# Input projection by Strassen's algorithm: seven products per pair of feature tiles, in three token passes

## What is computed

```python
h = rmsnorm(x, norm_w)
q, k, v, z_a, xbc, z_b, dt_raw, g_a, g_b = jnp.split(h @ w_in, split_points(SPLITS), axis=-1)
...
xbc = causal_conv(xpad, conv_w, conv_b)      # 4 taps along the tokens, then silu
...
dt = jax.nn.softplus(dt_raw.astype(jnp.float32) + dt_bias.astype(jnp.float32))
acs = jnp.cumsum(dt * a, axis=2)
```

## Time and profile before

| | us |
|---|---|
| median of 3 runs | 2437.13 |
| lowest and highest | 2435.5, 2437.49 |
| the profiled execution | 2436.28 |
| its span, first to last instruction | 2434.6 |
| PE busy in the span | 2288.5 (94%) |
| DVE, ACT, POOL busy | 812.7, 831.1, 636.8 |

### The profile page before, as it was taken

How to read it: one execution, slowest core, us unless ns; L and a number is a source line. 1 busy time by engine, 2 the same in 40 slices (tenths; PEclk the granted TensorE clock), 3 DMA queues, 4 the chain that set the end, 5 groups by cost and what they waited for, 6 DMA issues and landing times. The chain is left out here.

```text
span 2434.6 us, 35230 instructions
## 1 busy us (share of the span) xinstructions
PE 2288.5 (94%) x12671; PEld 2062.2 (85%) x12671; DVE 812.7 (33%) x1504; ACT 831.1 (34%) x1925; POOL 636.8 (26%) x547
## 2 busy tenths in 40 slices
PE   6999999999999999999999679999946999996999
PEld 5999999999999999999999668888734878874887
DVE  4211100014444100100000065555517999973221
ACT  5211111124444211221111165555525666742010
POOL 3101011011011011010110055555517767760000
PEclk9999999999999999999999879999976999997999
DMA  4411121111121111211112964444345777735333
GB/s 165 89 72 54 71 71 71 71 70 71 64 77 71 71 70 62 88 54 71 70 71 82 67 165 109 106 120 120 87 118 147 188 195 197 203 104 173 130 129 99
DMA packets 281028, 250.09 MB, mean 103 GB/s; under 512 B 75209, under 2 KB 258361, under 8 KB 273785
## 3 DMA queue, kind: packets, MB, share of 16 engines
q1 hardware_dynamic: 278856, 248.79, 35.8%
q10 hardware_dynamic: 2112, 0.53, 0.1%
HBM read 158.48 MB, written 90.81 MB: 102 GB/s over the span
## 5 line engine op out<-in xcount | busy, mean ns | idle before, releaser
L74 PE MATMUL acc<-h_hi,w_hi 128*128 128x424 f32 (+1 forms) x2280 | 810.5, 355 | 10.2 <-DVE h_lo L561 7.8
L75 PE MATMUL acc<-h_lo,w_hi 128*128 128x424 f32 (+1 forms) x2280 | 807.3, 354 | 0.0
L76 PE MATMUL acc<-h_hi,w_lo 128*128 128x424 f32 (+1 forms) x2280 | 807.0, 354 | 0.0
L74 PEld LDWEIGHTS acc<-h_hi,w_hi 128*128 128x128 f32 x2280 | 430.2, 189 | 24.7 <-DVE h_lo L561 8.6
L332 POOL TENSOR_TENSOR w_lo<-w_raw,w_hi 128x1024 fp32r<-128x1024 f32 x57 | 144.7, 2539 | 1130.5 <-ACT w_hi L374 1130.5
L75 PEld LDWEIGHTS acc<-h_lo,w_hi 128*128 128x128 f32 x2280 | 430.6, 189 | 7.3
L76 PEld LDWEIGHTS acc<-h_hi,w_lo 128*128 128x128 f32 x2280 | 430.2, 189 | 7.3
L399 ACT ACTIVATE row<-acc 128x424 f32<-128x424 f32 (+1 forms) x215 | 112.7, 524 | 825.5 <-PE acc L76 825.4
L597 DVE SCALAR_TENSOR_TENSOR conv_acc<-conv_in,conv_wb,conv_acc 128x424 f32<-128x424 f32 (+2 forms) x216 | 126.1, 585 | 380.9 <-ACT conv_acc L444 373.1
L1120 ACT ACTIVATE a_prob<-a_score,a_neg_max 128x129 f32<-128x129 f32 x264 | 103.3, 398 | 45.9 <-DVE a_neg_max L1259 43.1
L74 PE MATMUL a_o_ps<-a_w_hi,a_at_hi 128*128 128x512 f32 (+1 forms) x272 | 117.0, 430 | 2.0 <-DVE a_branch L1292 2.0
(11 more groups left out here) (218 smaller groups left out, 3045.0 us busy)
## 6 DMA issues: line engine op xcount, KB each, us to landing
proj<-row SPq DMA_DIRECT2D x56, 1056.0 KB, 4.0
w_raw<-in_w_in_dram SPq DMA_DIRECT2D x28, 1024.0 KB, 5.2
s_feat<-proj SPq DMA_DIRECT2D x16, 1280.0 KB, 8.6
s_acs_b<-acs_dram SPq DMA_DIRECT2D x16, 1024.0 KB, 7.5
a_q_diag<-proj SPq DMA_DIRECT2D x66, 128.0 KB, 4.4
a_z<-proj SPq DMA_DIRECT2D x16, 512.0 KB, 4.7
a_gate_t<-proj SPq DMA_DIRECT2D x16, 512.0 KB, 4.6
branch_rows<-a_branch SPq DMA_DIRECT2D x16, 512.0 KB, 3.2
```

Source lines behind the costliest of these rows:

```text
L74: pe.matmul(out, hi, whi, start=first, stop=False)
L75: pe.matmul(out, hi, wlo, start=False, stop=False)
L76: return pe.matmul(out, lo, whi, start=False, stop=last)
```

## The change

The projection is rewritten. The 56 tiles without dt form 28 pairs. Tokens go in three passes (`PASSES`) of 704 columns, each of two sides of 352 (`NB`), and in each pass all 28 pairs are worked through, so the weights are loaded three times. For a pair the product is seen as a 2 by 2 block product: two feature tiles, two halves of the 1024 input features, two token sides. Seven block products (`PRODUCTS`, j = 0 to 6) take the place of eight, each over 4 slices of input features, so 12 matmuls of 352 columns. Their left operands are quarters of the weights or sums of them (`ws`, and one in place in `w_raw`), their right operands quarters of h or sums of them (h in `hraw`, sums in `t2`, `t3` and in place), split into `hh` and `hl` once a pass. The products run into four PSUM banks:

```diff
+            def product(n, j):
...
+                bank, first = [(x_ps, True), (q_ps, True), (x_ps, False), (z_ps, True), (x_ps, False), (z_ps, False),
+                               (r_ps, True)][j]
+                pe.wait_ge(wlo_ready, PRODUCTS * n + j + 1)
+                if i == 0:
+                    pe.wait_ge(hlo_ready, PRODUCTS * p + j + 1)
+                if j == 0:
+                    after(pe, part_copied, 4 * n)
+                if j in (2, 4, 5):
+                    pe.wait_ge(part_copied, 4 * n + {2: 1, 4: 2, 5: 3}[j])
+                if j in (1, 3, 6):
+                    after(pe, summed, 4 * (n - 1) + {1: 1, 3: 3, 6: 4}[j])
+                more = not first
+                out = bank[:, 0:NB]
+                for k in range(4):
+                    pe.matmul(out, wh[:, j, k], hh[:, j, k], start=first and k == 0, stop=False, skip_group_check=more)
+                    pe.matmul(out, wh[:, j, k], hl[:, j, k], start=False, stop=False, skip_group_check=more)
+                    mm = pe.matmul(out, wl[:, j, k], hh[:, j, k], start=False, stop=k == 3, skip_group_check=more)
+                mm.then_inc(product_done, 1)
-            def tile(T, slot, query=False, extra=None):
-                pe.wait_ge(wlo_ready, T + 1)
-                for b in range(UNITS):
-                    pe.wait_ge(evacuated, UNITS * T - UNITS + b + 1)
-                    products(b, slot, range(KT)).then_inc(unit_done, 1)
```

ACT copies four partial results of a pair out of PSUM (`copy_part`, after products 0, 2, 3 and 4), and DVE adds them to banks (`total_of`, and one subtraction in SBUF). Every one of the seven left operands has one buffer, is rounded by ACT (`split_hi`, 512 elements) and completed by POOL (`split_lo`). The order of ACT and DVE in pair n, without what concerns single pairs:

```diff
+                copy_part(n, 0)
+                if last in func:
+                    function_row(n - 1, 0, func[last])
+                if last == "conv":
+                    tap0(n - 1, 0)
+                high(0)
+                if prepared(n) is not None:
+                    square(prepared(n))
+                if last == "conv":
+                    conv_silu(n - 1, 1)
+                high(1)
+                if n and prepared(n - 1) is not None:
+                    h_copy(prepared(n - 1), 0)
+                    h_copy(prepared(n - 1), 1)
+                copy_part(n, 1)
+                high(2)
+                if last == "conv":
+                    conv_silu(n - 1, 0)
+                copy_part(n, 2)
+                high(3)
...
+                copy_part(n, 3)
+                high(4)
+                high(5)
+                if kind in func:
+                    function_row(n, 1, func[kind])
+                if kind == "conv":
+                    tap0(n, 1)
+                high(6)
...
+                if last == "query":
+                    square_row(n - 1)
+                if last == "conv":
+                    taps(n - 1, 1)
+                if n + 1 < ALL:
+                    weight_sums(n + 1)
+                if prepared(n) is not None:
+                    normalise(prepared(n))
+                if last == "conv":
+                    taps(n - 1, 0)
+                free_target(n, 0)
+                total_of(n, 0, 0, q_ps, P1, 1, 1)
...
+                free_target(n, 1)
+                total_of(n, 1, 0, z_ps, U2, 5, 2)
+                dve.wait_ge(part_copied, 4 * n + 4)
+                dve.tensor_tensor(P4, U4, P4, ALU.subtract).then_inc(u_minus_p, 1)
+                dve.wait_ge(u_minus_p, n + 1)
+                total_of(n, 1, 1, z_ps, P4, 5, None)
...
+                total_of(n, 0, 1, r_ps, U4, 6, 4)
```

More of the change, by code:

```diff
@@ L131, in project_inputs @@
[L131 to L141, removed]
+        qs = pb("qs", [P, 2, BANK])
+        xflat = xbuf[:, :, :].rearrange("p a n -> p (a n)")
@@ L189, in rows_of @@
[L189 to L212, removed]
+        zeroed = sem("zeroed")
@@ new lines, in project_inputs, with kind_of, column @@
+        Q_PAIRS, CONV_FIRST, CONV_PAIRS = 4, 10, 6
+        PREP = [6, 7, 8, 9, 16, 17, 18, 19]
+        DT_PAIR = 21
+        LAST = PAIR_COUNT - 1
+        def kind_of(i):
+            if i < Q_PAIRS:
+                return "query"
+            if i < 6:
+                return "copy"
+            if i < CONV_FIRST or 16 <= i < 20:
+                return "silu"
+            return "conv" if i < 16 else "sigmoid"
+        def column(i):
+            return 2 * P * i if i < 20 else COL_G + 2 * P * (i - 20)
@@ L474, in _ @@
-            evacuate_first(0, UNITS - 1)
-            split_hi(2, 0, 0, 2)
-            evacuate_first(1, UNITS - 2)
-            evacuate_first(1, UNITS - 1)
-            act.wait_ge(params, 16 * (2 * TAPS))
-            act.wait_ge(hist_zero, 1)
-            for first, last, kind in segments():
-                with act.Fori(max(first, 1), min(last, pairs - 1)) as p:
-                    for s in range(2):
-                        T = 2 * p + s
-                        split = (T + 1, 1 - s, 1 - s, p + 1 + s)
-                        if kind == "conv":
-                            conv_tile(T, s, p, split)
-                        else:
-                            plain_tile(T, s, p, ACT.Silu if kind == "silu" else ACT.Copy, split, kind == "query")
@@ new lines, in free_target @@
+            def free_target(n, f):
+                kind = kind_of(n % PAIR_COUNT)
+                if kind in ("query", "copy"):
+                    after(dve, stored[n % 2], 16 * (n // 2))
+                    return
+                before = kind_of((n - 1) % PAIR_COUNT)
+                if before in ("silu", "sigmoid"):
+                    dve.wait_ge(row_ready, rows_before(n) - (0 if f == 0 else 1))
+                if before == "conv":
+                    q = n - 1
+                    dve.wait_ge(tap0_ready, taps_before(q, f, len(tap_pieces(q // PAIR_COUNT))))
+                    dve.wait_ge(carried, q // PAIR_COUNT * 2 * CONV_PAIRS + 2 * (q % PAIR_COUNT - CONV_FIRST) + 2 - f)
```

999 lines of the change are left out of this document (574 added, 425 removed).

## The result

The changed kernel takes **2475.78 us** (median of 4, 2472.84 to 2477.68) against 2437.31 (2435.5 to 2437.77): a ratio of 1.0156, 95% interval 1.014 to 1.0172. It is 38 us slower, where 13 were forecast. Its profiled execution took 2472.84 us with a span of 2471.1; before these were 2436.28 and 2434.6. The second stage starts at 1416.95 instead of 1381.18, and what follows takes as long as before (1054.15 against 1053.4). So all of it is in the projection, 35.8 us, of which the sum had forecast 13.3.

What follows compares the result with a forecast made beforehand. PE alone was taken to bound the projection. Start 66, 83 pairs 1120.5, narrow work 36, conv pairs 133, turns 21, tails 12 and end 6 made 1394.5 us against 1381.2, so 2450 us in all; range 2400 to 2490.

Steps and rivals of the forecast that it cites:

- conv pairs: Pairs with convolution taps on DVE, 18 in three passes: PE idles ahead of product 5 and loses clock, 133 us together.
- start: Setup through pair 0, with all 8 token tiles turned before product 0: pair 0 ends at about 66 us, bounds 60 and 72.
- Interval of a matmul: PE's time per 352-column matmul in the projection: 160.7 ns, making 84 pairs 172 us less than before.
- Rival 3: Matmul time beyond columns at 2.4 GHz all but vanishes for shorter matmuls, 1.0 us in each of 66 pairs: 2384 us, chance 0.04.
- The walk: One conv pair followed through DVE, ACT and PE: product 5 waits for z_ps's copy, 18.8 instead of 13.5 us.
- I take 1.2: 22 us: Clock loss on PE behind each conv pair stall: 1.2 us each, between 0 and 1.7, 22 us in all.
- Rival 2: PE stays at half clock through both products behind each conv stall, 3.9 us lost instead of 1.2: 2498 us, chance 0.08.
- Rival 1: POOL's low-part splits fall into gaps of DVE, so the conv term falls by 36 us: 2411 us, chance 0.30.
- Tails: Six single-value stores hold SP ahead of pair 77's weight load: stall about 9.5 us, 12 with clock, bounds 0 and 25.
- it lands some 12 later: Pair 77's weight load: SP reaches it 30 us after pair 74 starts, and it lands some 12 us later, at 42.
- first transposes about 11, then ACT at 2.2 us a tile: Setup before product 0: turning all 8 token tiles takes until about 29 us.
- Rival 4: Other pairs also wait a little, for low parts or a late copy, 0.5 us in 60 pairs: 2480 us, chance 0.11.

Runs made afterwards that it cites:

- e_all3: e_all2 with e_order3's order on ACT, softplus in three groups, and POOL's low parts of pair 0 held until the last token tile is normalised: 2376.5 us.
- e_order3: Changed kernel with both silus of a conv pair behind the copies PE waits for, and z_ps's copy ahead of the third weight operand's rounding: 2414.7 us.
- e_soft: Changed kernel with the 16 softplus steps on DVE spread four each over the ends of pairs 3 to 6 of the last pass: 2464.5 us.
- e_all2: Changed kernel with both silus behind the copies, tail stores spread over six pairs, softplus in four groups, and token-tile normalisation at its pair's end: 2384.1 us.
- e_order3_lock: e_order3 with POOL's low parts of pairs 11 to 17 of each pass cut to 32 of 512 elements, the rest left out: 2326.2 us.

## Why the prediction was wrong in size

It forecast slower by 13 us and got slower by 38; the stage missed its sum by 22.5 us (1417.0 for 1394.5). The direction came out of the right mechanism. The size failed in five places. Three terms were too small: the conv pairs (by their clock, 9 us in all), the load that lands behind the tails (9) and the start (6.5). Two were put at nothing: the softplus (9.0) and the held normalisations (3.8).

- **Interval of a matmul:** 158.9 ns instead of 160.7, within its bounds of 158.3 and 162.3, and 12 us to the good. Rival 3 fell. By the isolated gap in the Trainium skill (TensorE: Matmul & The Clock Gate, Back-to-back issue gap) the estimate would be 149.2; the measurement decides, as at 512 columns.
- **Conv pairs:** 142.1 instead of 133. The walk held almost to the tenth: 5.1 us idle for 5.3, 3.9 us of holds for 4.0, released by the copy of z_ps. PE's idle time in the 18 pairs sums to 100.8 us where the walk had 111 (63.7 for 67 in the first two passes, 37.1 for 44 in the last). The step that failed is the clock, "I take 1.2: 22 us". Beyond the pace and the idle time the pairs took 41 us, 19 more, which the shorter idle time half made up for: product 5 lost 1.7 us behind nearly every stall, the upper bound of the prediction, and product 6 up to 1.0 more in pair 16 and in three pairs of the last pass. Rival 2 (both products at half clock, 3.9 us a stall) fell by these rows. Rival 1 (low parts in gaps of DVE) fell: the short low parts gave 90 us, the forecast had 72 and some clock.
- **Tails, the term most off for its size:** 20.8 instead of 12. The step "it lands some 12 later" failed. SP was free of the stores after 25.65 us, as the earlier trace rows had it, but then the load's own issue took 6.71 us, and ACT could use its data 21.6 us after that issue began.
- **Start:** 72.5 instead of 66 (before, the first product ran at 26.44). The step "first transposes about 11, then ACT at 2.2 us a tile" took a plain normalisation of the last tile; it was held 4.7 us by POOL behind a power. e_all3 gave 4 to 5 of it back. And the copy of z_ps stood behind a rounding, worth 4.8 as e_order3 shows.
- **Softplus, missing:** 9.0. The prediction gave DVE 12.7 of 13.5 us in a query pair and didn't ask what else the list puts there. 16 dependent operations took 13.4 us (983.97 to 997.4). Moving them gave back 7.0 of the 9.0 (e_soft). In the kernel before, DVE stands at 0 to 4 tenths in slices 2 to 22 and PE at 9 throughout, so there such a block costs PE nothing that shows:

```profile
DVE  4211100014444100100000065555517999973221
```

- **Held normalisations, missing:** 3.8. The prediction charged 1.5 us for one in pair 16 and nothing for the others. The ones ahead of pairs 19 and 20 read 4.79 and 6.07 us instead of 1.28. In e_all2 and e_order3_lock those within the passes read 1.27 or 1.28 and these pairs take 14.1 us, but both kernels differ in more, so this cause is likely and not shown alone.
- **Turns and narrow work:** 19.2 for 21, 34.3 for 36. The end 6.1 for 6.

The misses in start, conv, tails, softplus and normalisations sum to 37 us and all point one way, and the pace gave back 12.4. Each of the four besides conv is work that was free under a DVE or an SP with slack, in a kernel whose change had used that slack up. Rival 4 (a little lateness in every other pair) fell too: plain pairs take 13.35 us and PE waits for nothing in them.

## What to carry to other kernels

Fewer matmuls paid for by more vector work pay off only where the vector engines keep room in every pair, not on average; here 18 of 84 pairs had none. When a change takes an engine's slack, go through its list once and ask of each block of work that was free before what it now delays: the chain in one pair, the burst of small stores, the setup. And on an engine that issues in order, put the copy that another engine waits for ahead of everything that itself waits; it was worth 53 us here for one moved line.

## What the hardware showed

- Behind a power on POOL (0.55 us), an operation of DVE with two SBUF inputs waited for the whole row of POOL operations that followed without a gap: 8.38 us for one that reads 1.28 alone, beside six that take 7.36. Without the power, or with a gap behind it, it waited for one (2.27 to 2.38 us). Each case was run once. What holds it is not settled. The Trainium skill (SBUF — State Buffer, SBUF: two separate sides) states the exclusion as a lock that the first one holds for a whole instruction; the probes without a power agree, with 1.73 us for an operation of 0.69, and the 8.38 us are not in that rule.
- Six stores of single values in a row held the DMA issue on SP for 25.65 us. One in each of six pairs held it 0.47 us five times, and 3.36 the last time.
